# A decoder layer on eight cores: two programs with a join rewritten as one program with host-arranged operands

## The reference

```python
hcat = x @ w_in[i]                                   # (B, S, 3584)
b_gate, c_gate, hc, q, k, v, g = jnp.split(hcat, split_at, axis=-1)
y_conv = b_gate * causal_short_conv(c_gate * hc, conv_w[i])   # (B, S, 512)
q = rotary(q.reshape(bsz, s, RET_HEADS, RET_HEAD_DIM), positions)
k = rotary(k.reshape(bsz, s, RET_HEADS, RET_HEAD_DIM), positions) * (RET_HEAD_DIM ** -0.5)
o = chunkwise_retention(q, k, v)                     # (B, S, H, D), 16 chunks of 128
y_ret = jax.nn.silu(g) * head_group_norm(o, ret_gn_w[i], ret_gn_b[i])
mix = jnp.concatenate([y_conv, y_ret], axis=-1) @ w_out[i]
x = layer_norm(DEEPNORM_ALPHA * x + mix, ln1_w[i], ln1_b[i])
ff = jnp.square(jax.nn.relu(x @ w_ff1[i])) @ w_ff2[i]
ple = jax.nn.sigmoid(x @ w_ple_gate[i]) * (p[i] @ w_ple_proj[i])
x = layer_norm(DEEPNORM_ALPHA * x + ff + ple, ln2_w[i], ln2_b[i])
```

## Time and profile before

| | us |
|---|---|
| median of 6 runs | 1072.49 (1069.82 to 1077.14) |
| the profiled execution's own time | 1072.97 |
| its span (first to last instruction of the slowest core, core 0) | 1071.4 |
| spans of the eight cores | 1056.7 to 1071.4 |
| PE busy in the span | 881.7 (82%) |
| DVE, ACT, POOL busy | 494.5, 299.5, 181.0 |

### The profile page before, as it was taken

One profiled execution on the slowest core, in us unless ns is written; L12 is line 12 of the kernel. 1 busy time (PEld: TensorE's weight loads), 2 busy tenths in 40 slices (PEclk: granted clock), 3 DMA queues, 4 the chain that ended last, 5 costly groups with the idle time before them and its releaser, 6 DMA issues.

```text
span 1071.4 us, 14470 instructions; the slowest of 8 cores (1056.7 to 1071.4 us)
## 1 busy us (share of the span) xinstructions
PE 881.7 (82%) x4762; PEld 435.3 (41%) x4762; DVE 494.5 (46%) x781; ACT 299.5 (28%) x469; POOL 181.0 (17%) x251
## 2 busy tenths in 40 slices
PE   2689799785785637999999989999989999999990
PEld 2534345554452322434443334444334444334440
DVE  1236556764763562335514645423635432654105
ACT  1212322341431263331322331322331231432001
POOL 6100006647772222000010000010100010000001
PEclk9689999997996868999999999999999999999995
DMA  9999957999996207535362534461543551551412
GB/s 191 225 154 127 99 61 78 104 95 81 93 84 178 80 1 197 186 121 223 128 206 65 190 139 179 168 213 40 176 178 114 201 176 73 191 212 66 156 41 79
DMA packets 84753, 143.86 MB, mean 134 GB/s; under 512 B 48420, under 2 KB 66888, under 8 KB 74440
## 3 DMA queue, kind: packets, MB, share of 16 engines
q0 software_dynamic: 66896, 38.28, 29.6%
q1 hardware_dynamic: 16416, 101.72, 27.1%
q10 hardware_dynamic: 1368, 2.94, 0.9%
HBM read 164.42 MB, written 29.36 MB: 181 GB/s over the span
## 4 chain that ended last, share of the span: by engine, by line
PE 48%; issue 4%; DVE 4%; ACT 3%; DMA 2%; POOL 0%; ACTq 0%; DVEq 0%; SPq 0%; POOLq 0%
PE pF L182 38%; PE pm L182 7%; PE pT L186 2%; DMA cslab<-s_ff 2%; ACT tR L209 1%; DVE ubuf L189 1%; DVE acc L189 1%; DVE hT L189 1%; ACT x1b L209 1%; DVE lnst L232 0%; ACT pT L209 0%; ACT ubuf L209 0%; ACT ffs L209 0%; DVE ubuf L200 0%; DVE lnst L236 0%
## 5 line engine op out<-in xcount | busy, mean ns | idle before, releaser
L182 PE MATMUL pF<-ycat,kslab 128*128 128x512 bf16 x992 | 225.6, 379 | 12.8 <-ACT tR L209 6.9
L182 PE MATMUL pF<-hT,cslab 128*128 128x512 bf16 x1024 | 229.2, 381 | 6.8 <-DMA cslab<-s_ff 6.8
L182 PEld LDWEIGHTS pF<-ycat,kslab 128*128 128x128 bf16 x992 | 90.1, 97 | 146.9 <-issue 56.9
L182 PEld LDWEIGHTS pF<-hT,cslab 128*128 128x128 bf16 x1024 | 99.8, 98 | 121.2 <-issue 10.1
L189 DVE TENSOR_TENSOR hT<-pF,tR 128x512 bf16<-128x512 f32 x128 | 88.2, 689 | 123.5 <-ACT tR L209 118.6
L182 PE MATMUL pf<-xT,wsl 128*128 128x128 bf16 (+1 forms) x896 | 120.8, 298 | 21.0 <-DVE vz L189 13.8
L209 ACT ACTIVATE tR<-pF 128x512 f32<-128x512 f32 x128 | 76.2, 595 | 146.2 <-PE pF L182 129.6
L182 PE MATMUL pm<-kslab,ycat 128*128 128x512 bf16 x448 | 103.7, 383 | 0.0
L189 POOL TENSOR_TENSOR lnst<-lnst,neghalf 128x1 f32<-128x1 f32 x28 | 15.4, 551 | 508.5 <-DVE lnst L193 508.5
L182 PE MATMUL pf<-wsl,xT 128*128 128x512 bf16 x384 | 85.6, 379 | 18.6 <-ACT wsl L209 17.0
L182 PEld LDWEIGHTS pf<-xT,wsl 128*128 128x128 bf16 x896 | 70.1, 102 | 70.8 <-issue 29.4
(11 more groups left out here) (114 smaller groups left out, 888.7 us busy)
## 6 DMA issues: line engine op xcount, KB each, us to landing
cslab<-s_ff SPq DMA_DIRECT2D x32, 1024.0 KB, 6.3
kslab<-s_ff SPq DMA_DIRECT2D x31, 1024.0 KB, 6.7
s_ff<-w_ff POOLq DMA_DIRECT2D x16, 1024.0 KB, 22.9
ycat<-x SPq DMA_DIRECT2D x16, 512.0 KB, 9.4
kslab<-s_gate SPq DMA_DIRECT2D x8, 1024.0 KB, 5.4
out<-acc POOLq DMA_DIRECT2D x16, 512.0 KB, 4.4
kslab<-s_wout SPq DMA_DIRECT2D x6, 1024.0 KB, 4.8
xin<-x SPq DMA_DIRECT2D x12, 512.0 KB, 5.3
```

What stands on the lines that cost most here:

```text
L182: self.P.op("pe", lambda e: e.matmul(out, lhsT=lhsT, rhs=rhs, start=start, stop=stop), reads, writes)
```

## The change

The whole kernel is written anew as one program without a join in the middle.

- **Operands.** The host hands over x transposed in four tiles (`xT`), p transposed, and every weight slab laid out as it will lie in SBUF; all stay float32. POOL's queue casts x tiles, conv slabs (`wc`) and q, k, g straight into SBUF, in the order in which conv wants them. No transpose of x or p is left on PE. w_v comes in float32 by SP and DVE takes its mean per head out (`center_v`), so that o has no mean and the group norm needs only squares, summed by ACT. Decay is put on v, so that q needs no scale and the state is gathered in PSUM, multiplied once in four chunks.
- **Retention.** A step t does v, q, k of chunk t, transposes and scores and o of chunk t-1, norm and y of t-2. The gate g is made per head for 512 tokens (`do_g`). One bank `psT` serves all transposes. w_out and LN1 of tile 0 stand in steps 8 to 13, seven FF1 groups in steps 14 to 17.
- **FFN.** FF1 has three banks and three `tR`; FF2 has tokens as rows, four banks over 8 slabs, and adds straight to the accumulator, with no transposes. The last half of FF2 goes block by block, each with its norm and store. One ring of six buffers takes all slabs. SBUF bytes are reused by hand (`place`).

```diff
-            def load_wj(i, j):
-                h.dma("pool", wsl[i][:, :, j * 128:(j + 1) * 128],
-                      w_in[:, i * 512 + j * 128:i * 512 + (j + 1) * 128].rearrange(
-                          "(kc p) n -> p kc n", p=128),
-                      ("wslj", i, j), [], [("wslj", i, j)])
...
+        def cast(dst, src, key, res):
+            h.dma("pool", dst, src, key, [], [res])
...
+        cast(xT[0][:], xTd[0], ("xT", 0), ("xT", 0))
+        cast(wc[0][:], wcd[0], ("wc", 0), ("wc", 0))
+        cast(wc[1][:], wcd[1], ("wc", 1), ("wc", 1))
+        cast(xT[1][:], xTd[1], ("xT", 1), ("xT", 1))
+        cast(wc[2][:], wcd[2], ("wc", 2), ("wc", 2))
+        cast(wc[3][:], wcd[3], ("wc", 3), ("wc", 3))
+        cast(xT[2][:], xTd[2], ("xT", 2), ("xT", 2))
+        cast(xT[3][:], xTd[3], ("xT", 3), ("xT", 3))
+        for i, (t, n) in enumerate(((wG, "wG"), (wQ, "wQ"), (wK, "wK"))):
+            cast(t[:], wqkvg[i], n, n)
+        h.dma("sp", wVf[:], wqkvg[3].rearrange("p a (h e) -> p (a h) e", e=128), "wVf",
+              [("wc", 1)], ["wVf"])
...
+        casts = []
+        for g in range(2):
+            casts.append((s_wout[g], w_out[g], ("c_wout", g), ("s_wout", g)))
...
+        for g in range(8):
+            casts.append((s_ff2[g], w_ff2[g], ("c_ff2", g), ("s_ff2", g)))
...
+        def center_v():
+            for k in range(4):
+                sl = slice(k * 8, (k + 1) * 8)
+                h.red(vmean[:, sl], wVf[:, sl, :], ["wVf"], ["vmean"])
...
+        for tt, j in ((0, 0), (0, 1), (1, 0), (1, 1), (0, 2), (1, 2), (0, 3), (1, 3)):
+            conv(tt, j)
+        bg.add(center_v())
+        for tt in (2, 3):
...
+        def do_v(n):
+            b = proj(n, wV, "wV")
+            c = n % 4
+            h.tt("dve", f4(vb[n % 2][:]), f4(ps[b][:]),
+                 vsc[:, 4 * c:4 * c + 4].unsqueeze(2).broadcast_to([128, 4, 128]), ALU.mult,
+                 [RP[b], "cst"], [("vb", n % 2)])
...
+            for kc in range(8):
+                h.mm(ps[b][:], wG[:, kc, hh * 128:(hh + 1) * 128], xT[tt][:, kc, :],
+                     kc == 0, kc == 7, ["wG", ("xT", tt)], [RP[b]])
+            h.act(gs[tt % 2][:, hh, :], ps[b][:], AF.Silu, [RP[b]], [("gs", tt % 2, hh)])
...
+            h.cp("act", qkT[n % 2][:], psT[:], [RT], [("qkT", n % 2)])
...
+            for hh in range(4):
+                e_ = slice(hh * 128, (hh + 1) * 128)
+                h.act(sqj[:], ps[O_PS][:, e_], AF.Square, [RP[O_PS]], ["sqj", ("st4", i)],
+                      scale=float(128.0 ** -0.5), accum=st4[:, i, hh:hh + 1])
...
-                for kc in range(8):
-                    bank = pf[b0 + kc // 4]
-                    h.tr(bank[:, (kc % 4) * 128:(kc % 4 + 1) * 128],
-                         xb[blk % NXB][:, kc * 128:(kc + 1) * 128], identf[:],
-                         [r_xb, "identf"], [PF[b0 + kc // 4]])
...
-            for i in range(3, 7):
-                load_w(i)
...
-                casts.append((s_ff2[c], w_ff2[:, c * 128:(c + 1) * 128].rearrange(
-                    "(fc p) n -> p fc n", p=128), "s_cast", ("s_ff2", c)))
...
+        def mix_part(tt, bi, hf, slab, rs, bank):
...
+            h.dma("sp", xin[i][:], x[b * 128:(b + 1) * 128, cols], ("xin", i), [], [("xin", i)])
+            for kc in range(8):
+                h.mm(ps[bank][:], ycat[:, kc, blk(b)], slab[:, kc, :], kc == 0, kc == 7,
+                     [("ycat", b), rs], [RP[bank]])
+            h.stt(x1v(tt, bi)[:, cols], xin[i][:], ALPHA, ps[bank][:], ALU.mult, ALU.add,
+                  [("xin", i), RP[bank]], [x1r(tt, bi)])
...
+        def load_slab(src, rsrc):
+            i = rcnt[0] % NR
+            rcnt[0] += 1
+            h.dma("sp", ring[i][:], src, ("ring", i), [rsrc], [("ring", i)])
+            return ring[i], ("ring", i)
...
+        def ff1_group(tt, bank):
+            fc = ff1["n"] % 32
+            if fc % 4 == 0:
+                ff1["slab"] = load_slab(s_ff1[fc // 4], ("s_ff1", fc // 4))
+            slab, rs = ff1["slab"]
+            f = fc % 4
...
+            for kc in range(8):
+                h.mm(ps[bank][:], slab[:, kc, f * 128:(f + 1) * 128],
+                     ycat[:, kc, tt * 512:(tt + 1) * 512], kc == 0, kc == 7, [rs] + ycr(tt), [RP[bank]])
+            t, rt = tR[i], ("tR", i)
+            h.act(t[:], ps[bank][:], AF.Relu, [RP[bank]], [rt])
+            h.tt("dve", hT[:, fc, :], ps[bank][:], t[:], ALU.mult, [RP[bank], rt], [("hT", fc)])
...
+        for t in range(NB + 2):
+            if t < NB:
+                do_v(t)
+            elif t == NB:
+                ff1_group(0, next_bank())
...
+            if 0 <= t - 1 < NB:
+                do_scores(t - 1)
+            bg.step()
+            if t + 2 < NB:
+                do_g(t + 2)
+            elif t <= NB:
+                ff1_group(0, next_bank())
+            bg.step()
+            if 10 <= t < 14:
+                bg.until(chains[t - 10])
+                x1_transpose(0, t - 10)
+            if 0 <= t - 1 < NB:
+                do_o(t - 1)
+            bg.step(2)
...
+                slabs0 = [load_slab(s_wout[g], ("s_wout", g)) for g in range(2)]
+            if 8 <= t < 12:
+                bi = t - 8
+                for hf in range(2):
+                    mix_part(0, bi, hf, slabs0[hf][0], slabs0[hf][1], next_bank())
+                    bg.step()
+                chains.append(gen_ln1(0, bi))
+                bg.add(chains[bi])
+            issue_casts(1)
...
+        def phase_ff1(tt):
+            while ff1["n"] < 32 * (tt + 1):
+                ff1_group(tt, bank3())
+                bg.step(2)
...
-            def P4g(n):
-                for hh in range(4):
-                    for kc in range(8):
-                        h.mm(v_ps[:, hh * 128:(hh + 1) * 128], wG[:, kc, hh * 128:(hh + 1) * 128],
-                             xT[:, kc, ctok_(n)], kc == 0, kc == 7, [("wsl", 6), rx(n)], [rv])
-                h.act(gsr[n % 2], f4(v_ps[:]), AF.Silu, [rv], [("gsr", n % 2)])
...
-                h.red(sum4, o4, [ro], [rsa])
-                h.act(sq, o4, AF.Square, [ro], ["sq"])
-                h.red(ssq4, sq, ["sq"], [rsb])
...
-            P1(0)
-            for t in range(NB + 4):
-                drain = t >= 15
-                if ok(t):
-                    E1(t)
...
-                if ok(t - 3):
-                    P4g(t - 3)
-                    P4(t - 3)
-                    E4a(t - 3)
-                    E4b(t - 3)
...
-                if ok(t + 1):
-                    P1(t + 1)
-                issue_casts(1)
...
-            P.join_all()
-            P.emit(st, "a", st0)
...
-            def next_F():
-                i = fcnt[0] % 2
-                fcnt[0] += 1
-                return pF[i], RF[i], i
...
+        def phase_ff2(tt):
+            for hf in range(2):
+                if tt == 3 and hf == 1:
+                    slabs = [load_slab(s_ff2[4 + g], ("s_ff2", 4 + g)) for g in range(4)]
+                    for bi in range(4):
+                        for g in range(4):
+                            ff2_mm(bi, hf, g, *slabs[g])
+                            bg.step(3)
+                        ff2_add(tt, bi, hf)
+                        bg.add(gen_out(tt, bi))
+                    continue
+                for g in range(4):
+                    slab, rs = load_slab(s_ff2[hf * 4 + g], ("s_ff2", hf * 4 + g))
+                    for bi in range(4):
+                        ff2_mm(bi, hf, g, slab, rs)
+                        bg.step(2)
+                        if g == 3:
+                            ff2_add(tt, bi, hf)
...
+        for tt in range(4):
+            phase_ff1(tt)
+            bg.flush()
+            phase_gate(tt)
+            if tt < 3:
+                phase_mix(tt + 1)
+                bg.add(gen_norm1(tt + 1))
+            phase_ff2(tt)
+            bg.flush()
+            if tt < 3:
...
-                def fin(c, i):
-                    for bi in range(4):
-                        h.tr(pT32[:, bi * 128:(bi + 1) * 128], ffs[i][:, bi * 128:(bi + 1) * 128],
-                             identf[:], [("ffs", i), "identf"], [RT32])
-                    h.tt("dve", a4[:, :, c * 128:(c + 1) * 128],
```

More of the change, by code:

```diff
@@ L37, in __init__, with place, _take_over @@
         self.written = set()
-        self.alias = {}
-        self._alias_seen = set()
+        self.places = {}
+        self.live = []
+        self.dead = set()
+    def place(self, res, lo, hi):
+        self.places[res] = (lo, hi)
+    def _take_over(self, r):
+        if r not in self.places or r in self.live:
+            if r in self.dead:
+                raise RuntimeError("resource used after its bytes were taken: %r" % (r,))
+            return []
+        if r in self.dead:
+            raise RuntimeError("resource used after its bytes were taken: %r" % (r,))
+        lo, hi = self.places[r]
+        over = [q for q in self.live if self.places[q][0] < hi and lo < self.places[q][1]]
+        for q in over:
+            self.live.remove(q)
```

(62 more changed lines are left out.)

1116 lines of the change are left out of this document (423 added, 693 removed).

## The result

The changed kernel takes 904.2 us, median of 10 runs, against 1072.86 of the kernel before beside it (20 runs): ratio 0.8424, 95% interval 0.8406 to 0.8441. Faster, as forecast, and inside the range of 835 to 925, but 39 us above the likeliest 865 and above its own range of 840 to 890. In the profiled execution the cores of one die ran at a lower clock, so every row of after is of core 0 on the other die, whose span is 904.3 us; the medians here count such executions, the ratios leave them out.

A forecast was written before the change was run, and what follows sets the result against it. Limits differed by stage: transfers in conv, waits in the retention, PE busy in the FFN; the gain was put in waits. Start 16, conv 87, retention 178, FFN 567, end 15 sum to 863 us, 865 with 1.6; range 835 to 925.

The forecast's parts named there:

- PE floor of 792 us: Whole program: 3520 matmuls of 512 columns take 760 us, 568 of 128 columns 32 us.
- The queue: Rival: POOL's one casting queue is the bound, at 46 GB/s, giving 1148 us, slower than before; chance 0.04.
- the clock: Rival: PE's clock falls as PE gets dense; all 792 us at 0.87 gives 983 us; chance 0.06.
- a chain: Rival: retention steps stay at 11.05 us across PE, DVE, POOL and ACT, 219 us not 178, total 906; chance 0.20.
- the signs: Expected in the profile: first conv matmul at 14 to 20 us, clock at 0.97 or more from 110 us on, among others.
- Start and conv: First matmul at 16 us, bounds 10 and 22; conv then 87 us, ending at 103 us.
- Retention: Sixteen chunks plus moved-in work: PE 162.9 us, waits of 6, 6 and 3, so 178 us; FF weight casts cost nothing.
- FFN: PE 546 us, plus LN2 9, late slab 7 and clock 5: 567 us in all; 148 us per tile.
- LN2 beside FF1: LN2 of the tile before shares DVE with FF1: 3 us in each of three tiles, 9 us.
- The late FF2 slab: FF2's first slab stands behind the x loads on SP's queue: 3 x 2.2 us, 7 us.
- End: After the last matmul one block's add, norm and store plus the join remain: 15 us, 12 to 19, against 26.
- Nothing waits: Rival: every stage takes the ends of its bounds, total 827 us; chance 0.10.

The follow-up runs named there:

- experiment 6: Changed kernel with 4 KB cast rows, whole x rows in tile 0, new SP and ring order, FF2's first slab ahead of x loads: 857.7 us, ratio 0.803.
- experiment 10: Changed kernel with two PSUM banks in FF1 in place of three, nothing else: 912.5 us, ratio 0.8547.

## Why the prediction was right, and where its size was off

**The mechanism held, the sum lacked a term.** The measured time lies in the stated range because that range was wide: it was set for other cases than the one that came. The gain was put in waits, stage by stage, on a PE floor of 792 us. PE is busy 806 in the changed kernel (overlapping) and 800 in that of experiment 6, whose three stages have no wait above 2.7 us behind the first matmul. The queue did not become the bound, the clock stayed at 0.94 to 1.00 in the stages with matmuls, and the retention did not stay a chain: steps are 9.35 to 9.6 us apart, not 11.05. That 906 stood as the price of the chain is a coincidence; the 904 come about in another way. (Its 219 us are 16 x 11.05, the 27.7 moved in, and all 15 us of the forecast's waits; with those of LN alone, as it is worded, it is 211 and the sum 898.) Of the signs, the first matmul at 20.26 and a clock of 0.94 in the retention lie just outside.

**Start and conv: right in sum.** First matmul at 20.26, forecast 16 with bounds 10 and 22; conv then takes 84.2 us, forecast 87, and ends at 104.5, forecast 103. PE waited for the first cast and then never again up to the retention's first chunk.

**Retention: the step that failed.** It was "a cast a chunk is 10.3 us of queue at 102 GB/s, about the chunk's own length, and the last lands at about 290, FF2 wants it after 355". Its numbers are fair: outside steps 8 to 13 the FF weights' casts are issued 9.3 to 10.5 us apart, the last at 303. What it priced at nothing is what they do to SP's loads beside them. The casts fill the engines for most of the time from the start to about 340 us, when p's weights have landed, and I looked for their bytes and their deadline, not for the loads that share the engines with them. The term should have been two holes: 24.9 us in the retention (211.6 against 185.0 in experiment 6, whose stretch ends eight matmuls, 1.7 us, sooner) and, before FF1's third slab, 12.3 of waiting with 2.5 of slow matmuls behind it (9.55 us against 7.07). The step that made them meet was in my own list: w_out of tile 0 is "moved in here", into the retention, and I counted its matmuls. Its x, w_out and LN1 loads moved too, from behind the issue of the last cast into the middle of the casts, whose packets the change had made 32 KB long.

Beside that, 186.7 without the holes is 9 above 178. Waits come to 24 us over the floor of 162.9, not 15: in experiment 6 five waits for DVE or ACT beside LN1 are 1.1 to 1.9 us each, where I took 1.

**FFN: right in sum, 569.5 for 567, by errors that cancel, which is luck.** LN2 beside FF1 was 9 us and is nothing (experiment 10 shows the third bank paying for it). The late FF2 slab was 3 x 2.2 and waited 1.80, 2.17 and 2.62, with 1.7 and 1.6 us of slow matmuls behind the last two (8.75 and 8.62 against 7.07); the period of a tile was 148 and is 145.7 and 147.8 (405.54, 551.25, 699.08). The third slab of FF1 filled the gap, 14.8. Without any late load the stage takes 547.6 with those eight matmuls of the retention, 545.8 without, against a floor of 546.

**End: 18.7 for 15.** The last block's add begins 2.7 us after the last matmul (885.6), at 888.28, since DVE is still in the norm of the block before; the trace shows its last pass from 887.14. I had counted one block and not the one that ends just ahead of it.

**The rivals.** "Nothing waits" was 827; experiment 6, which has no late load, is at 857.7: the rest are the 24 us of small waits in the retention, the start and the end. The clock never cost what that case needed.

## What to carry over

When a change turns small transfers into large ones on one queue, price it for the other queues too: count the packets that carry data per queue in a stretch, look at their size, multiply by the time of the other queue's packet, and compare with the moment at which a load is wanted. A background stream that fills the DMA engines is not free because its own deadline is far; shorter packets help the loads beside it until the stream itself becomes late (here 4 KB was better than 32, 2 and 1). And a wait of 2 us in front of a dense stretch of matmuls can cost 4, when the matmuls behind it run at the lower clock for a while.
